# A hybrid decoder layer on one Trainium2 core: adaLN row sums on VectorE, a load order turned over five pairs, and a reordered ending

## The chip, the core and the metric

The kernel runs on one core of a Trainium2 chip. The core has five engines that run their own instruction streams and meet at semaphores: TensorE (PE, matrix products, with PEld for its weight loads), VectorE (DVE), ScalarE (ACT), GpSimd (POOL) and SyncE (SP, which here only issues DMAs). Sixteen DMA engines move data between HBM and the on-chip memory SBUF; products land in PSUM, which has eight banks of 512 float32 per partition. The metric is the device time of one execution in microseconds (us). Lower is better.

## What is computed

One decoder layer on 256 tokens of width 1024, float32 throughout. All weights are read once from HBM. Cut to what matters:

```
mod = c @ w_ada + b_ada                       # six rows of 1024: sh1, sc1, gt1, sh2, sc2, gt2
h = rms_norm(x, g1) * (1 + sc1) + sh1
proj = h @ w_in                               # DeltaNet q/k/v, z, FoX q/k/v, two gates
y_a = gated_deltanet(proj) @ w_o_delta        # chunked recurrence, 4 heads, 4 chunks of 64
y_b = forgetting_attention(proj) @ w_o_fox    # 4 heads
x = x + gt1 * ((sig(gate_a) * y_a + sig(gate_b) * y_b) @ w_out)
h2 = rms_norm(x, g2) * (1 + sc2) + sh2
x = x + gt2 * experts(h2)                     # router, top 4 of 32, clamped SwiGLU
out = rms_norm(x, g_final)
```

The conditioning `mod` has three parts of 2048 columns each, called ada0, ada1 and ada2 in the kernel: ada0 is sh1 and sc1, ada1 is gt1 and sh2, ada2 is sc2 and gt2. Each expert has 8 MB of gate and up weights and 4 MB of down weights, so the 32 experts are 403 MB of the 463 MB that are read.

## The kernel before

The order of all work is written by hand, one block of code for each engine. There is a first phase (to about 320 us), in which the layer up to the router is computed, and an expert phase.

**First phase.** The weights come through a ring of eight slots of 1 MB (`NSTREAM`), in the order of the list `UNITS`. `stream(n)` on SP issues the load of unit n once the unit that was in its slot has been used (`unit_used`, counted by PE). The list before: ada0 (8 units), dn (6), fqk (4), fv (2), z (2), ada1 (8), gates (8), ada2 (8), wo_fox (2), wo_delta (2), w_out (4). PE computes a conditioning part with `ada(part, b, ks)`: four products of 512 columns for each unit, with c copied into 32 columns as the weights, into four quarters of bank b. DVE then copies the bank (`take_mod_rows`), PE transposes the copy (`mod_transposes`), and DVE adds the bias (`take_mod`).

Projections (`project`) take a unit as two halves. For most units ACT rounds the weights (`w_hi`, line 1097), POOL computes the remainder (`w_lo`, line 1787, one operation of 128x1024 for each half, both inputs in SBUF), and PE makes three passes. DVE meanwhile does the convolution of the dn units, the decay and softmax biases, the scaling of q and k (lines 1448 and 1450) and the decay masks (lines 1457 and 1458, then `dec_ready`). PE waits for `dec_ready` before it transposes v (line 683), and after that projects z. Then come `chunk_pairs`, the triangular inverse by five levels with half a gates projection in each gap, and the recurrence over four chunks. The recurrence has more PE work in its gaps: `between_state` and `between_vnew`, the last three of which are ada2. After it, four calls of `out_branch` for wo_fox, four for wo_delta, and the product with w_out.

**Expert phase.** Experts go in pairs; pair I has experts 2I (par 0) and 2I+1 (par 1). PE, for each expert: gate and up products (`gate_up`, 8 units of 1 MB, lines 944 and after), transposes of the activation, then `down` in two halves of 2 MB. The gate and up weights have 16 slots (8 for each par), the first down half one place for each par, and the second half ("high", slots 18 and 19) one place that every expert uses in turn. SP's order of loads follows `by_place` up to pair 9: four gate-up loads of 2 MB, the first down half, and after them the high half of the expert before, since its place comes free last. From pair `TURN + 1 = 11` it follows `by_need`, where the high half of an expert comes directly behind its first half. Pair 10 is written out as the turn. Each load waits for its place to be free (`gu_used`, `dn_used`), and SP issues strictly in order.

**The ending.** `last_pair` multiplies the last expert's down weights into PSUM bank 6 after DVE has taken the expert before out of that bank (`y_moved`). `last_scatter` adds the last pair to the tokens. Then the final norm: ACT squares and roots, DVE one reciprocal and two products of 128x512 for each half of the tokens (line 1775), and ACT issues the four stores (line 1328).

## Time and profile before

| | us |
|---|---|
| median of three runs | 1239.37 |
| lowest, highest | 1239.18, 1241.2 |
| the profiled execution, its own time | 1238.21 |
| span of the profiled execution | 1236.4 |
| PE busy | 1138.6 (92%) |
| DVE busy | 316.1 (26%) |
| ACT busy | 184.7 (15%) |
| POOL busy | 106.0 (9%) |
| DMA | 464.7 MB, mean 376 GB/s |
| chain that ended last | PE 64%, DMA 29%, issue 3%, ACT 2%, DVE 2% |

The span is what lies between the first and the last instruction of the profiled execution, 1.8 us less than that execution's own time and 3.0 us less than the median. Times in rows are counted from the start of the span. "Idle before" is what an engine stood still for before a row's first instruction, with the name of what ended it. PE's clock as granted was 0.984 of full speed on average.

### The profile page before, as it was taken

The page shows a single profiled execution, that of the slowest core. Times are in us where ns is not written, and L with a number is a line of the kernel's source. Part 1 is how long each engine was busy: PE and PEld are TensorE (multiplying, and loading weights), DVE is VectorE, ACT ScalarE, POOL GpSimd, SP SyncE. Part 2 cuts the span into 40 slices and gives each one's busy share as a digit, 9 for nine tenths or more (in the row PEclk, how much of TensorE's full clock was granted, in tenths as well). Part 3 has the DMA queues.
Part 4 walks back from the last instruction along what each step waited for, and adds up shares of the span by engine and source line. Part 5 has one row for each costly group of instructions (what it writes and reads, how often), then busy time and mean ns, then how long its engine had stood idle before and what let it go on. Part 6 is the DMA issues. An engine that isn't in the chain of part 4 may idle for free.

```text
span 1236.4 us, 15283 instructions
## 1 busy us (share of the span) xinstructions
PE 1138.6 (92%) x6307; PEld 585.6 (47%) x6307; DVE 316.1 (26%) x674; ACT 184.7 (15%) x316; POOL 106.0 (9%) x50
## 2 busy tenths in 40 slices
PE   5999999999999999998989889898999999999896
PEld 2999799688543334333333323333434333333322
DVE  1633562131421221221212212121221222122102
ACT  2476344101310000010100000000000000000001
POOL 0764443110000000000000000000000000000000
PEclk9999999999999999999989999999999999999999
DMA  9963763597999999999999999999989999999995
GB/s 352 335 222 107 249 219 103 170 422 310 376 420 426 429 428 429 428 429 428 429 429 428 428 428 428 429 428 429 429 368 430 428 429 428 429 428 428 429 426 245
DMA packets 62558, 464.70 MB, mean 376 GB/s; under 512 B 8469, under 2 KB 31130, under 8 KB 34618
## 3 DMA queue, kind: packets, MB, share of 16 engines
q1 hardware_dynamic: 61256, 462.13, 90.9%
q10 hardware_dynamic: 1218, 1.93, 0.5%
q8 instruction: 26, 0.43, 0.1%
q0 software_dynamic: 48, 0.13, 0.0%
q14 instruction: 10, 0.08, 0.0%
HBM read 463.13 MB, written 1.05 MB: 375 GB/s over the span
## 4 chain that ended last, share of the span: by engine, by line
PE 64%; DMA 29%; issue 3%; ACT 2%; DVE 2%; SPq 0%; ACTq 0%; DVEq 0%
PE ps L488 61%; DMA ring<-in_w_down_dram 22%; DMA ring<-in_w_gate_up_dram 6%; PE ps L940 1%; ACT kept L1291 1%; DMA ring<-in_w_in_dram 1%; DMA ring<-in_g_onorm_dram 1%; PE ps L972 0%; PE ps L496 0%; ACT w_hi L1097 0%; DVE ring L1491 0%; SPq L358 0%; DVE ring L1485 0%; DVE ring L1775 0%; DVE kept L1717 0%
## 5 line engine op out<-in xcount | busy, mean ns | idle before, releaser
L488 PE MATMUL ps<-ring,kept 128*64 128x512 f32 (+1 forms) x3040 | 657.8, 600 | 36.1 <-DMA ring<-in_w_down_dram 22.5
L488 PEld LDWEIGHTS ps<-ring,kept 128*64 128x64 f32 (+1 forms) x3040 | 212.2, 138 | 454.3 <-issue 400.8
L488 PE MATMUL ps<-kept 128*128 128x128 f32 (+4 forms) x984 | 193.9, 413 | 8.5 <-ACT kept L1291 3.3
L488 PEld LDWEIGHTS ps<-kept 128*128 128x128 f32 (+2 forms) x984 | 108.5, 177 | 96.1 <-issue 81.0
L1287 ACT ACTIVATE kept<-kept 128x512 f32<-128x512 f32 x32 | 20.1, 629 | 731.4 <-DVE kept L1694 731.4
L1717 DVE TENSOR_TENSOR kept<-ps,kept 64x512 f32<-64x512 f32 x64 | 44.0, 688 | 298.4 <-PE ps L488 297.4
L1694 DVE TENSOR_SCALAR kept<-ps 128x512 f32<-128x512 f32 x32 | 22.1, 691 | 382.4 <-PE ps L488 382.4
L1787 POOL TENSOR_TENSOR w_lo<-ring,w_hi 128x1024 fp32r<-128x1024 f32 x38 | 91.8, 2434 | 108.2 <-ACT w_hi L1097 108.2
L488 PE MATMUL ps<-hT_hi,w_hi 128*128 128x256 f32 x272 | 78.7, 289 | 0.0
L488 PE MATMUL ps<-ring 64*64 64x64 f32 (+6 forms) x784 | 74.8, 270 | 3.0 <-issue 3.0
L488 PE MATMUL ps<-hT_lo,w_hi 128*128 128x256 f32 x272 | 77.0, 283 | 0.0
L488 PE MATMUL ps<-hT_hi,w_lo 128*128 128x256 f32 x272 | 76.9, 283 | 0.0
L488 PEld LDWEIGHTS ps<-ring 64*64 64x64 f32 (+3 forms) x784 | 65.4, 159 | 12.8 <-issue 6.9
L488 PE MATMUL ps<-kept,ring 128*128 128x256 f32 (+1 forms) x252 | 56.2, 381 | 4.7 <-DMA ring<-in_w_in_dram 2.6
L488 PEld LDWEIGHTS ps<-kept,ring 128*128 128x128 f32 x252 | 47.1, 195 | 12.3 <-issue 3.3
L488 PEld LDWEIGHTS ps<-hT_hi,w_hi 128*128 128x128 f32 x272 | 52.1, 192 | 0.5
L488 PEld LDWEIGHTS ps<-hT_lo,w_hi 128*128 128x128 f32 x272 | 52.1, 192 | 0.1
L488 PEld LDWEIGHTS ps<-hT_hi,w_lo 128*128 128x128 f32 x272 | 52.1, 192 | 0.0
L1097 ACT ACTIVATE w_hi<-ring 128x1024 fp32r<-128x1024 f32 x38 | 39.2, 1053 | 49.2 <-PE ps L488 37.1
L940 PE MATMUL ps<-kept 128*128 128x128 f32 x128 | 21.7, 292 | 22.6 <-issue 22.6
L940 PEld LDWEIGHTS ps<-kept 128*128 128x128 f32 x128 | 19.1, 206 | 33.4 <-issue 29.3
L1291 ACT ACTIVATE kept<-ps 128x512 f32<-128x512 f32 x32 | 19.1, 597 | 85.7 <-PE ps L940 85.7
(227 smaller groups left out, 513.8 us busy)
## 6 DMA issues: line engine op xcount, KB each, us to landing
ring<-in_w_gate_up_dram SPq DMA_DIRECT2D x127, 2048.0 KB, 26.4
ring<-in_w_down_dram SPq DMA_DIRECT2D x47, 2048.0 KB, 23.8
kept<-in_w_down_dram SPq DMA_DIRECT2D x16, 2048.0 KB, 24.0
ring<-in_w_ada_dram SPq DMA_DIRECT2D x24, 1024.0 KB, 5.0
ring<-in_w_in_dram SPq DMA_DIRECT2D x22, 1024.0 KB, 11.5
ring<-in_w_out_dram SPq DMA_DIRECT2D x4, 1024.0 KB, 16.3
ring<-in_w_o_fox_dram SPq DMA_DIRECT2D x2, 1024.0 KB, 9.8
ring<-in_w_o_delta_dram SPq DMA_DIRECT2D x2, 1024.0 KB, 12.8
```

The source lines that it names most:

```text
L488: return pe.matmul(dst, lhsT, rhs, start=start, stop=stop, skip_group_check=True)
L940: last = pe.transpose(bank(7, kk * P, P), fours[:, kk, :], ident)
L1097: A(hi_buf_r(n)[:, :, cols], w[:, :, cols], ACT.Copy).then_inc(S("split_hi"), 1)
L1287: A(sig_a, gate_a, ACT.Sigmoid, scale=ALPHA).then_inc(S("sig_ready"), 1)
L1291: A(act_t_last if par == 0 and not more else act_t, bank(7), ACT.Copy).then_inc(S("act_t_ready"), 1)
L1694: TS(gate_a, bank(4), LIMIT, None, ALU.min).then_inc(S("gate_ready"), 1)
L1717: TTn(ypair[par * 64:par * 64 + 64, d * 512:(d + 1) * 512], ps[64 * d:64 * d + 64, 6, :], gt2_row[64 * d:64 * d + 64, d * 512:(d + 1) * 51 ...
L1787: pool.tensor_tensor(lo_r[:, :, cols], lo[:, :, cols], hi_buf_r(n)[:, :, cols].bitcast(F32), ALU.subtract).then_inc(S("split_lo"), 1)
```

## The change

Conditioning. The eight units of ada1 and of ada2 are no longer multiplied by PE. DVE builds a sum over them (`add_rows`): a unit of 128x2048 times c as a scalar for each partition, added to `ada_sums[part]`, sixteen operations in all, of which the first of each part is a product alone. Each counts `ada_used`. PE then adds the 128 rows with four products against a matrix of ones (`ada_over_rows`, counts `ada_summed`), one for each quarter of the bank. The units of ada1 and ada2 are spread over the list `UNITS` from the third dn unit to the z units, and a slot that held one is released by `ada_used`. `mod_transposes(1)` moves ahead of the chunk pairs, and the one of ada2 from behind the recurrence to ahead of the levels, which now wait for `mod_cols_taken` 3. The gaps of the recurrence that held ada2 hold the first two `fox_branch` calls.

Load order. `next_expert(I, i, par, late)` replaces `by_place` and `by_need`: `late` says behind how many loads of this expert the high half of the expert before is placed. It is 5 up to pair 8 and then 4, 3, 2, 1, 0, 0 for pairs 9 to 14.

Ending. The last expert's down goes to bank 4, with a wait for `gate_up_taken` in place of `y_moved`. In the final norm one of the four quarters is multiplied by g_final before its root is there and scaled by ACT; three stores go out from SP and one from ACT. Some semaphores are merged, without an effect on the order.

The diff, cut to its core:

```diff
-        UNITS += [("dn", u, win_unit(256 * u)) for u in range(6)]
...
-        UNITS += [("ada1", k, ada_unit(1, k)) for k in range(KD)]
...
+        UNITS += [dn(0), dn(1), dn(2), ada(1, 0), dn(3), dn(4), ada(1, 1), dn(5), fox(0), ada(1, 2), ada(1, 3)]
+        UNITS += [fox(1), fox(2), ada(1, 4), ada(1, 5), ada(1, 6), fox(3), ada(1, 7), ada(2, 0), fox(4), ada(2, 1)]
+        UNITS += [ada(2, 2), fox(5), ada(2, 3), ada(2, 4), zz(0), ada(2, 5), zz(1), ada(2, 6), ada(2, 7)]
...
-                    sp.wait_ge(S("unit_used"), n - NSTREAM + 1)
+                    sp.wait_ge(S("ada_used" if SUMMED[n - NSTREAM] else "unit_used"),
+                               USED_AT[UNITS[n - NSTREAM][0:2]])
...
+            def next_expert(I, i, par, late, first_unit_whole=True):
...
+                for u in range(4):
+                    if u == late:
+                        high_of_last()
...
+                next_dn(I, i, par, 0)
+                if late == 5:
+                    high_of_last()
...
+                for i, late in zip(range(TURN, PAIRS - 1), (4, 3, 2, 1, 0, 0)):
...
+            def ada_over_rows(part, b):
+
+                pe.wait_ge(S("ada_used"), KD * part)
+                for q in range(4):
+                    last = mm(ps[32 * q:32 * q + 32, b, :], km("ones")[:, 0:32],
+                              ada_sums[part][:, 512 * q:512 * q + 512], True, True)
+                last.then_inc(S("ada_summed"), 1)
...
+            def add_rows(part, k):
...
+                if k == 0:
+                    last = TS(ada_sums[part], unit_sb(n), vec("c", k), None, ALU.mult)
+                else:
+                    dve.wait_ge(S("ada_used"), KD * (part - 1) + k)
+                    last = STT(ada_sums[part], unit_sb(n), vec("c", k), ada_sums[part], ALU.mult, ALU.add)
...
-                pe.wait_ge(S("y_moved"), i * 4 + 2)
-                down(i, 1, high, last_of=q)
+                pe.wait_ge(S("gate_up_taken"), i * 4 + 4)
+                down(i, 1, high, last_of=q, to=4)
...
+            act.wait_ge(S("norm_steps"), 4)
+            link(A(x2[:, 1, 0:512], x2[:, 1, 0:512], ACT.Copy, scale=oss[:, 1, 1:2]))
+            act.dma_start(out[0, P:2 * P, 0:512], x2[:, 1, 0:512]).then_inc(S("out_done"), 16)
```

**On DVE, before the decay masks.** The rows stand between the copy of the cumulated decays (128x48) and the first decay mask. `ring<-ring,kept 128x2048` is `add_rows`; a semaphore in brackets is what the instruction waits for, `slot_in` for a load. Before:

```order
L1429 COPY kept<-ps 128x48 [waits cums_ps]
L1436 SCALAR_TENSOR_TENSOR kept<-ps,kept,ring 128x128 [waits cums_ps,cums_taken]
L1438 SCALAR_TENSOR_TENSOR kept<-ps,kept,ring 128x256
...
L1448 SCALAR_TENSOR_TENSOR ring<-ring 128x1024 [waits qk_rstd,rowF_taken]
L1450 TENSOR_TENSOR ring<-ring 128x1024 [waits qk_rstd]
L1457 SCALAR_TENSOR_TENSOR ring<-ps,kept,ring 128x128 [waits cums_ps,unit_qk]
```

Now:

```order
L1474 COPY kept<-ps 128x48 [waits cums_ps]
L1427 SCALAR_TENSOR_TENSOR ring<-ring,kept 128x2048 [waits ada_used,slot_in5]
L1427 SCALAR_TENSOR_TENSOR ring<-ring,kept 128x2048 [waits ada_used,slot_in6]
...
L1427 SCALAR_TENSOR_TENSOR ring<-ring,kept 128x2048 [waits ada_used,slot_in1]
L1424 TENSOR_SCALAR ring<-ring,kept 128x2048 [waits slot_in2]
L1427 SCALAR_TENSOR_TENSOR ring<-ring,kept 128x2048 [waits ada_used,slot_in4]
...
L1427 SCALAR_TENSOR_TENSOR ring<-ring,kept 128x2048 [waits ada_used,slot_in0]
L1498 SCALAR_TENSOR_TENSOR ring<-ring 128x1024 [waits qk_rstd,rowF_taken]
L1500 TENSOR_TENSOR ring<-ring 128x1024 [waits qk_rstd]
```

Three operations of 128x2048 now stand ahead of the softmax biases (128x128 and 128x256), and six between them and the scaling of q and k.

**On PE, from the end of the z projections to the inverse's levels.** `128x12`, `128x64` and the `128x128` beside them are `mod_transposes`, `64x64` the chunk pairs, `32x512` a product with a conditioning unit or sum. Before:

```order
L488 MATMUL ps<-ring 64x64 [waits tok_taken]
...
L488 MATMUL ps<-ring,kept 32x512 [waits slot_in6,rowF_taken]
L488 MATMUL ps<-ring,kept 32x512 x3
L488 MATMUL ps<-ring,kept 32x512 [waits slot_in7]
...
L513 MATMUL ps<-kept 128x12 [waits run_in,mod_rows_sb]
...
L700 MATMUL ps<-kept,ring 128x128 [waits X1_ready]
```

Now:

```order
L536 MATMUL ps<-kept 128x12 [waits run_in,mod_rows_sb]
...
L503 MATMUL ps<-ring 64x64 [waits tok_taken]
...
L503 MATMUL ps<-ring,kept 32x512 [waits ada_used,mod_cols_taken]
L503 MATMUL ps<-ring,kept 32x512 x3
...
L725 MATMUL ps<-kept,ring 128x128 [waits X1_ready]
...
L538 MATMUL ps<-kept 128x128 [waits mod_rows_sb]
...
L503 MATMUL ps<-ring 128x128 [waits U_ready,M_ready,attn_ready,mod_cols_taken]
```

The 32 products of ada1 are gone from between the pairs and the transposes of X, the first half gates projection stands there in their place, and the first level waits for the conditioning's last part.

**On PE, at the end of the recurrence.** `128x256` from `ring` alone is an `out_branch`. Before:

```order
L488 MATMUL ps<-ring,kept 32x512 [waits slot_in6,obT_ready]
...
L488 MATMUL ps<-ring 64x128 [waits state_ready]
...
L488 MATMUL ps<-ring,kept 32x512 [waits slot_in1]
...
L488 MATMUL ps<-ring 128x256 [waits proj_taken,slot_in7,slot_in6]
L488 MATMUL ps<-ring 128x256 x7
L515 MATMUL ps<-kept 128x128 [waits mod_rows_sb]
```

Now:

```order
L503 MATMUL ps<-ring 128x256 [waits slot_in7,proj_taken,slot_in6,obT_ready]
L503 MATMUL ps<-ring 128x256 x7
L503 MATMUL ps<-ring 64x128 [waits state_ready]
...
L503 MATMUL ps<-ring 128x256 [waits proj_taken,slot_in7,slot_in6]
L503 MATMUL ps<-ring 128x256 x7
L503 MATMUL ps<-ring 128x128 [waits vnew_ready]
L503 MATMUL ps<-ring 128x128 x3
L503 MATMUL ps<-ring 128x256 [waits slot_in7,slot_in6,yb_taken]
```

Two of the four branches with wo_fox have moved into the gaps of the recurrence, where ada2 stood.

## Rows read from the trace of the kernel before

**Rows 1.** Windows: length; PE, PEld, DVE, ACT, POOL busy; PEclk, DMA share, GB/s

```profile
241.00:301.50 60.50, 57.51 (x286) 48.39 (x279) 16.11 (x31) 2.82 (x11) 7.79 (x5) 0.97 1.01 411
301.50:311.00 9.50, 9.50 (x58) 8.15 (x57) 1.77 (x5) 3.12 (x6) 0.00 (x0) 1.00 0.02 7
311.00:485.00 174.00, 165.24 (x822) 69.86 (x822) 45.87 (x123) 21.22 (x43) 1.60 (x2) 1.00 1.00 422
485.00:886.00 401.00, 365.84 (x1690) 142.33 (x1686) 84.19 (x189) 27.69 (x56) 0.00 (x0) 0.97 1.01 429
...
914.00:922.00 8.00, 8.00 (x40) 2.67 (x38) 2.78 (x7) 0.00 (x0) 0.00 (x0) 1.00 0.54 188
```

**Rows 2.** Timeline of SP's issues (start, us, count)

```profile
266.05 45.02 SPq L358 DMA_DIRECT2D ring<-in_w_gate_up_dram  x8
...
918.85 0.33 SPq L373 DMA_DIRECT2D ring<-in_w_down_dram  x1
```

**Rows 3.** Timeline of DVE, 24 to 124 us

```profile
24.65 2.29 DVE L1351 TENSOR_TENSOR kept<-kept 128x2048 f32<-128x2048 f32 x1 [9.57 <-ACT kept L1083]
...
94.51 0.21 DVE L1429 COPY kept<-ps 128x48 f32<-128x48 f32 x1 [0.62 <-PE ps L488]
100.74 0.35 DVE L1436 SCALAR_TENSOR_TENSOR kept<-ps,kept,ring 128x128 f32<-128x128 f32 x1 [6.02 <-PE ps L488]
...
116.90 1.23 DVE L1448 SCALAR_TENSOR_TENSOR ring<-ring 128x1024 f32<-128x1024 f32 x1 [13.46 <-ACT ring L1174]
...
123.18 0.34 DVE L1458 SCALAR_TENSOR_TENSOR ring<-ps,kept,ring 128x128 f32<-128x128 f32 x1
```

**Rows 4.** Timeline of POOL

```profile
93.38 5.03 POOL L1787 TENSOR_TENSOR w_lo<-ring,w_hi 128x1024 fp32r<-128x1024 f32 x2 [1.07 <-ACT w_hi L1097]
109.32 4.77 POOL L1787 TENSOR_TENSOR w_lo<-ring,w_hi 128x1024 fp32r<-128x1024 f32 x2 [10.92 <-ACT w_hi L1097]
118.76 9.82 POOL L1787 TENSOR_TENSOR w_lo<-ring,w_hi 128x1024 fp32r<-128x1024 f32 x4 [4.67 <-ACT w_hi L1097]
145.80 9.41 POOL L1787 TENSOR_TENSOR w_lo<-ring,w_hi 128x1024 fp32r<-128x1024 f32 x4 [17.23 <-ACT w_hi L1097]
...
178.92 5.22 POOL L1787 TENSOR_TENSOR w_lo<-ring,w_hi 128x1024 fp32r<-128x1024 f32 x2 [4.02 <-ACT w_hi L1097]
```

**Rows 5.** Timeline of DVE, products with both inputs in SBUF

```profile
124.35 1.89 DVE L1465 TENSOR_TENSOR kept<-kept 128x8 f32<-128x8 f32 x1 [0.83 <-issue]
...
178.38 3.51 DVE L1491 TENSOR_TENSOR ring<-ring 128x512 f32<-128x512 f32 x2 [0.84 <-PE ps L488]
```

**Rows 6.** Timelines of PE and ACT, 123 to 155 us

```profile
123.58 1.09 PE L683 MATMUL ps<-kept,ring 128*128 128x128 f32 x8 [1.37 <-DVE ring L1458]
...
136.11 2.08 PE L488 MATMUL ps<-ring 128*64 128x64 f32 x64
138.12 7.08 PE L488 MATMUL ps<-ring,kept 128*32 128x512 f32 x64
...
154.86 0.60 ACT L1131 ACTIVATE ring<-ps 128x512 f32<-128x512 f32 x1 [2.72 <-PE ps L488]
```

**Rows 7.** Timeline of PE, 234 to 259 us

```profile
234.84 2.78 PE L488 MATMUL ps<-ring,kept 128*32 128x512 f32 x24
237.55 1.96 PE L488 MATMUL ps<-ring 128*64 128x128 f32 x16
...
248.15 5.38 PE L488 MATMUL ps<-ring 128*128 128x256 f32 x16 [2.99 <-issue]
...
254.52 3.72 PE L488 MATMUL ps<-ring 128*128 128x256 f32 x16
```

**Rows 8.** Timeline of all engines, 1216 to 1233 us

```profile
1216.92 3.65 PE L488 MATMUL ps<-kept 128*64 128x512 f32 x16 [1.51 <-DVE kept L1717]
...
1221.69 0.14 PEld L488 LDWEIGHTS ps<-ring,kept 128*64 128x64 f32 x2 [0.29 <-DMA ring<-in_w_down_dram]
...
1230.79 1.41 DVE L1775 SCALAR_TENSOR_TENSOR ring<-ps,kept,ring 128x512 f32<-128x512 f32 x2
```

More of the change, by code:

```diff
@@ L281, in layer_kernel @@
         UNIT_AT = {(name, i): n for n, (name, i, _) in enumerate(UNITS)}
+        SUMMED = [name in ("ada1", "ada2") for name, _, _ in UNITS]
+        USED_AT = {(name, i): SUMMED[:n + 1].count(SUMMED[n]) for n, (name, i, _) in enumerate(UNITS)}
         WHOLE = 1
@@ L481, in _ @@
             sp.wait_ge(S("gu_used"), n * (16 * PAIRS) + (16 * PAIRS - 8))
[L482 removed]
+            sp.dma_start(flat[:, 0:1024], g_final.partition_broadcast(P)).then_inc(S("narrow_in"), 16)
+            for t, d, step in ((0, 0, 3), (0, 1, 5), (1, 1, 6)):
+                cols = slice(512 * d, 512 * d + 512)
+                sp.wait_ge(S("norm_steps"), step)
+                sp.dma_start(out[0, t * P:(t + 1) * P, cols], x2[:, t, cols]).then_inc(S("out_done"), 16)
         @block.tensor
@@ L497, in _, with ada @@
                 last.then_inc(S("x_t"), 1)
-            def ada(part, b, ks=range(KD)):
+            def ada(b, ks=range(KD)):
                 for k in ks:
-                    w = unit_arrived(pe, f"ada{part}", k)
+                    w = unit_arrived(pe, "ada0", k)
                     for q in range(4):
@@ L523, in _ @@
             pe.wait_ge(S("cb_ready"), 1)
-            ada(0, 4, range(2))
+            ada(4, range(2))
             pe.wait_ge(S("xsq_ready"), 1)
@@ L529, in _ @@
             last.then_inc(S("xss_ps"), 1)
-            ada(0, 4, range(2, KD))
+            ada(4, range(2, KD))
             mod_transposes(0, 6)
@@ L941, in act_transposes, with down @@
                 last.then_inc(S("act_t_ps"), 1)
-            def down(i, par, high, js=range(2), acts=None, last_of=None):
+            def down(i, par, high, js=range(2), acts=None, last_of=None, to=6):
                 e = i * 2 + par
@@ L1430, in _ @@
             ins.then_inc(S("cums_taken"), 1)
+            for k in range(4, 7):
+                add_rows(1, k)
             dve.wait_ge(S("cums_taken"), 1)
@@ L1440, in _ @@
             last.then_inc(S("rowF_taken"), 1)
+            add_rows(1, 7)
+            for k in range(5):
+                add_rows(2, k)
             dve.wait_ge(S("rowF_taken"), 1)
@@ L1480, in _ @@
             last.then_inc(S("tok_taken"), 1)
+            for k in range(5, KD):
+                add_rows(2, k)
+            take_mod_rows(1, 5)
+            take_mod(1, 6)
             dve.wait_ge(S("pairs_ps"), 1)
```

211 lines of the change are left out of this document (108 added, 103 removed).

## The prediction

> **What bounds the kernel now.** Read first where the DMA engines stand still. From 311 to 485 us they move 422 GB/s, from 485 to 886 us 429 GB/s at a share of 1.01 [rows 1], while PE has gaps: it is busy 365.84 of 401 us. The expert phase is therefore bound by the stream of weights, and PE's own work there costs nothing. The stream has two holes. One is before it: from 301.5 to 311 us the DMA share is 0.02 [rows 1]. SP has a batch of eight gate-up loads under way, from 266.05 to 311.07 us [rows 2]; the last two wait for PE to finish the product with w_out, as PE is busy all through the hole. All that comes later is a fixed number of bytes, so each us by which PE's first phase ends earlier or later moves the end by a us. The second hole is at 914 to 922 us, share 0.54 [rows 1]: (1.01 - 0.54) x 8 = 3.8 us, at the turn of the load order, and it ends when SP issues a high half at 918.85 us [rows 2]. Behind the last byte there is a tail that PE, DVE and ACT make. So three things count: the length of PE's first phase, the hole at the turn, the tail.
>
> **The first phase: DVE's new work.** The price of one addition of 128x2048 with two inputs in SBUF is 2.29 us, from a product of that size [rows 3]; a three-operand operation of 128x1024 takes 1.23 us [rows 3], which fits. The two operations of part start (one input) are not in the trace: 2.3 us if they run at the same pace, about 1.3 if at the double; I take 1.3. Sixteen operations are some 35 us, most of it where DVE is idle. Four of them lie between convolutions, one more or less fills a gap each, and nobody waits for DVE there. Three follow the copy at 94.51 us, which has 6.02 us of idle time behind it, and six follow the softmax biases, with 13.46 us of idle time [rows 3]. By their own length: from 94.7 us three additions (6.9), the biases (2.7), 2.3 + 1.3 + 4 x 2.3 = 12.8, scaling of q and k (2.4), masks (4.2) end at 123.7 us. Before, the masks end at 123.52 us [rows 3]. So if these operations ran alone, this would cost 0.2 us.
>
> They don't run alone. POOL has eight of its remainders just here: two from 93.38, two from 109.32, four from 118.76 us, 2.4 us each [rows 4]. DVE's products with both inputs in SBUF take turns with such a POOL operation. A product of 128x8 takes 1.89 us, from 124.35 to 126.24, in the middle of POOL's run of four [rows 5]; two of 128x512 take 3.51 us, where 2048 elements alone take 2.29, and POOL's pair beside them takes 5.22 us against 4.77 [rows 4, 5]. One waits for the whole of the other's operation, and neither gets two in a row while the other waits. No row shows the three-operand form with two SBUF inputs beside a working POOL; the two that bound it are that product (full turn-taking) and the same form at 116.90 us with POOL idle (none) [rows 3]. I take the turn-taking, since the inputs are the same two. The Trainium skill states this as a rule (SBUF — State Buffer, "Who interferes with whom"): a DVE instruction with two SBUF inputs and a GpSimd instruction that reads SBUF exclude each other for a whole instruction. By that rule the cost is the one taken here; the trace agrees for the two-operand form.
>
> The sum: DVE reaches its first addition at 94.7, when POOL's first operation has some 1.3 us left; the other seven come in between one by one, 7 x 2.37 = 16.6 us. Masks then end at 123.7 + 17.9 = 141.6 us instead of 123.52. PE waits for them (1.37 us already now [rows 6]), so its z projections start **18.1 us later**. Its clock falls after such a stop: behind a wait of 2.99 us a branch of 16 records takes 5.38 us and the same one later 3.72 [rows 7], so 1.7 us more. The four products for ada1 between the z units cost 7.08 / 8 = 0.9 us [rows 6]. Sum at the end of z: **+20.7 us**.
>
> **From z to the levels.** Now it takes from 136.1 us (the start of the pairs) to 154.8 us (ACT takes gates 0, the last PE work before the levels) [rows 6], 18.7 us, of which ada1 is 7.08. That goes, 0.9 for ada2's sum comes. But two waits come with it. The gates 0 and 1 units arrive earlier than now, so ACT and POOL split them directly behind z, not from 145.80 us [rows 4]: POOL's four operations then stand across DVE's four products of level 0 and X, which take turns with them. Each waits up to 2.4 us; X is ready some 3.3 us after PE's gates 0. And DVE copies ada2's sum only after level 1, the attention product and q's decay (about 4.3 us from X on), PE transposes it (1.2) and DVE takes it (0.4) before the first level may start, where PE has only 1 us of other work. My sum from z's end: transposes 1.6, pairs 2.1, sum 0.9, gates 0 5.9, wait 3.3, then 5.9, together 19.7 us. **+1.0 us.**
>
> **The recurrence and the branches.** From 234.84 us, the first piece of ada2, to the fourth branch, at which SP issues again (266.05), it is 31.2 us now [rows 2, 7]. In it: ada2 (7.1), the wait of 2.99 for wo_fox, the slow branch, the transposes. What is left is 4 branches x 3.72, 1.96 and 1.16 of recurrence, 1.04 of transposes: 19.0 us. The wait for wo_fox goes, as its slots are now freed by gates units. What is late next is the root of the recurrence's norm, some 4.3 us after the recurrence, and 5.6 us of branches cover it. **-12.2 us.**
>
> First phase in all: 20.7 + 1.0 - 12.2 = **+9.5 us**.
>
> **The turn.** Between two high halves there are six loads (29.3 us at 4.9 us each); a step of `late` makes it five, once for each pair. A pair is then 11 loads, 53.8 us, and PE's own pair of experts is about as long, so neither waits. The high place is free about 6 us after its last load landed, with four or five loads (20 to 25 us) still under way. So the hole goes: **-3.8 us**, bounded by 0.
>
> **The ending.** The last down no longer waits 1.51 us for DVE [rows 8]. Its last load still lands shortly before 1221.7 us [rows 8], which may take back a part: -1.2, between -0.3 and -1.5. In the norm, one of the four products of 0.7 us [rows 8] leaves the path, and the four stores are no longer issued one behind the other: -1.2, between -0.5 and -1.8.
>
> **Sum, the likeliest case.** +9.5 - 3.8 - 2.4 = +3.3 us, rounded up to +3.6 for waits too small to list. The profiled execution's span is 1236.4 us, its own time 1238.21, the median 1239.37. Against the median: **1243 us**. Its own range: the turn-taking may cost 13 to 20 us instead of 18, the rest 3 us either way: 1238 to 1248.
>
> **Rivals.**
> *Three-operand additions don't take turns with POOL.* Then z starts 0.2 to 1.5 us later; DVE still has three additions ahead of ada1's transposes, which makes PE wait some 1.5 us; X is still late against POOL. The levels start about 2 us later than now, and the sum is +2 - 12.2 - 3.8 - 2.4 = -16.4: **1223 us** (1219 to 1230). For it: no row shows the form beside POOL. Against it: the two-operand rows. It decides at the first addition behind 94.7 us: 2.3 us or about 3.6.
> *The turn has a hole of its own*, or leaves the old one. For it: SP issues strictly in order, and every step puts a wait for `dn_used` earlier. Against it: the loads under way. Then 1243 + 3.8 = **1247 us**.
> *The first phase doesn't count.* If the hole of 9.5 us before the stream could take up a later end of w_out, the change would give only turn and ending: 1239.4 - 6.2 = 1233 us. Against it: the last two loads of the batch wait for that very product, and the hole grows with it.
>
> **How the numbers follow.** Measurement of this kernel can tell about 0.2%, 2.5 us. Likeliest case 0.63 (of it slower 0.39, same 0.19, faster 0.05); additions without turns 0.23, faster; a hole at the turn 0.08, slower; first phase without effect 0.02, faster; 0.04 for what I don't see, half same, half slower. Faster 0.30, same 0.21, slower 0.49. The range of 8 in 10 takes in the middle of the second case: 1221 to 1248.
>
> **What would show it.** Right: additions of 2.3 us that measure 3.5 to 4.7 where POOL works; a PE wait of some 15 to 19 us before line 683's transposes; masks done near 141.6 us; levels near 176 us; gate-up batch done near 320 us; no window under a share of 0.95 between 330 us and the end of the stream. Wrong: additions that stay at 2.3 us at 95 to 130 us, a z start before 130 us, or a new wait of PE for down weights in pairs 9 to 14.

## The result, and the profile after

The changed kernel takes 1245.2 us in the median of 20 executions (1240.13 to 1248.22), the kernel before 1238.99 us (20 executions, 1237.37 to 1242.17). The ratio is 1.0046, with a 95% interval of 1.0036 to 1.0055: slower by 5.7 us by the ratio (the two medians lie 6.2 us apart), where the forecast was +3.6 us and 1243 us. The profiled execution took 1242.11 us with a span of 1240.1 us, 3.7 us more than the span of before (1236.4). It lies 3.1 us under its own median; why is one of the questions below.

The page's line of the chain that ended last says where the new time is. DVE's share was 2%, now it is 5%, and PE's is the same:

```profile
PE 64%; DMA 25%; DVE 5%; issue 3%; ACT 2%; ACTq 0%; SPq 0%; DVEq 0%
```

Windows of the changed kernel (length; PE, PEld, DVE, ACT, POOL busy; PEclk, DMA share, GB/s), against [rows 1]:

```profile
301.00:311.00 10.00, 10.00 (x61) 8.56 (x59) 1.75 (x4) 0.40 (x1) 0.00 (x0) 1.00 1.01 429
311.00:321.00 10.00, 9.52 (x60) 8.09 (x56) 1.45 (x4) 3.73 (x9) 0.38 (x1) 1.00 0.41 143
485.00:886.00 401.00, 371.56 (x1717) 144.03 (x1715) 82.93 (x185) 27.49 (x56) 0.00 (x0) 0.97 1.01 428
914.00:922.00 8.00, 7.70 (x37) 2.64 (x36) 0.05 (x1) 0.60 (x1) 0.00 (x0) 1.00 1.00 426
```

SP's batch of eight gate-up loads in the changed kernel (start, us):

```profile
273.88 45.12 SPq L373 DMA_DIRECT2D ring<-in_w_gate_up_dram  x8
```

The batch is done at 319.00 us against 311.07 in [rows 2], so the hole ahead of the stream of weights, in which the DMA engines stand nearly still, has moved from between 301.5 and 311 us to between some 313 and 319 us, and is shorter. Between 485 and 886 us the stream is what it was, and the hole at 914 to 922 us (share 0.54 in [rows 1]) is gone (1.00). The last load lands shortly before 1225.48 us, 3.8 us later than in [rows 8]: 7.9 us lost ahead of the stream, 4.1 won at the turn. The tail behind it is as long as before.

Where the 7.9 us come from. DVE in the changed kernel, 96 to 138 us, to be laid beside [rows 3]:

```profile
96.02 9.50 DVE L1427 SCALAR_TENSOR_TENSOR ring<-ring,kept 128x2048 f32<-128x2048 f32 x3
...
108.05 2.35 DVE L1427 SCALAR_TENSOR_TENSOR ring<-ring,kept 128x2048 f32<-128x2048 f32 x1
110.31 1.28 DVE L1424 TENSOR_SCALAR ring<-ring,kept 128x2048 f32<-128x2048 f32 x1
111.69 15.53 DVE L1427 SCALAR_TENSOR_TENSOR ring<-ring,kept 128x2048 f32<-128x2048 f32 x4
127.15 3.36 DVE L1498 SCALAR_TENSOR_TENSOR ring<-ring 128x1024 f32<-128x1024 f32 x1
130.43 3.36 DVE L1500 TENSOR_TENSOR ring<-ring 128x1024 f32<-128x1024 f32 x1
...
137.70 0.34 DVE L1508 SCALAR_TENSOR_TENSOR ring<-ps,kept,ring 128x128 f32<-128x128 f32 x1
```

POOL in the same stretch, against [rows 4]:

```profile
94.21 6.72 POOL L1845 TENSOR_TENSOR w_lo<-ring,w_hi 128x1024 fp32r<-128x1024 f32 x2 [1.57 <-ACT w_hi L1127]
111.29 6.95 POOL L1845 TENSOR_TENSOR w_lo<-ring,w_hi 128x1024 fp32r<-128x1024 f32 x2 [10.37 <-ACT w_hi L1127]
120.72 15.28 POOL L1845 TENSOR_TENSOR w_lo<-ring,w_hi 128x1024 fp32r<-128x1024 f32 x4 [2.49 <-ACT w_hi L1127]
```

An addition alone takes 2.35 us (108.05). Four of them from 111.69 us take 15.53, 3.88 each, and the scaling of k, 1.22 us alone, takes 3.36. POOL's operations stretch as well: four take 15.28 us where they took 9.82. The masks end at 138.04 us instead of 123.52, and PE has to wait for them and for what stands ahead of them:

```profile
133.84 0.47 PE L700 MATMUL ps<-kept,ring 128*128 128x128 f32 x1 [9.47 <-DVE ring L1500]
...
138.10 1.97 PE L706 MATMUL ps<-kept,ring 128*128 128x128 f32 x8 [2.29 <-DVE ring L1508]
...
166.53 1.09 PE L725 MATMUL ps<-kept,ring 128*128 128x128 f32 x8 [2.67 <-DVE ring L1551]
170.79 1.11 PE L538 MATMUL ps<-kept 128*128 128x128 f32 x4 [3.17 <-DVE kept L1403]
...
172.91 3.78 PE L503 MATMUL ps<-ring 128*128 128x128 f32 x16 [0.34 <-DVE kept L1394]
```

The last row is the first level of the inverse: 3.78 us for 16 products of 128x128, half as fast as before, when the same row was

```profile
154.66 1.95 PE L488 MATMUL ps<-ring 128*128 128x128 f32 x16
```

PE's clock is at its lower level there. The windows of the changed kernel over PE's waits show that:

```profile
124.00:134.00 10.00, 0.53 (x5) 0.33 (x4) 9.96 (x4) 2.79 (x5) 10.00 (x4) 0.68 1.05 372
134.00:139.00 5.00, 2.71 (x12) 2.31 (x13) 4.96 (x19) 0.92 (x1) 2.01 (x1) 0.50 0.60 190
139.00:146.50 7.50, 7.50 (x58) 7.37 (x60) 7.40 (x7) 2.42 (x4) 0.00 (x0) 0.85 0.00 0
146.50:153.40 6.90, 6.90 (x57) 5.93 (x51) 3.00 (x3) 0.56 (x2) 0.00 (x0) 1.00 0.88 268
153.40:163.90 10.50, 10.46 (x130) 9.09 (x130) 8.18 (x14) 5.66 (x7) 8.89 (x4) 1.00 1.02 320
163.90:173.00 9.10, 2.96 (x17) 2.21 (x17) 8.24 (x12) 0.59 (x1) 1.42 (x1) 0.76 0.34 122
173.00:186.00 13.00, 13.00 (x103) 12.61 (x104) 4.16 (x5) 2.14 (x3) 2.37 (x1) 0.78 0.00 1
```

A PEclk of 0.50 is 1.2 GHz, 1.00 is 2.4 GHz; values between are mixtures. There are two dips, one in and behind the waits for k and the masks (9.47 and 2.29 us) and one in and behind the two waits ahead of the levels (2.67 and 3.17 us). The second one was not in the forecast.

### The profile page after: what moved, and what is told of

It reads as the page before. It is cut to its first block, busy times and chain, and to the rows that moved or that the text cites. A ratio compares the mean times of both kernels' runs of the same rounds, so it can differ in the third digit from the quotient of the medians.

```text
span 1240.1 us, 14937 instructions
## 1 busy us (share of the span) xinstructions
PE 1134.3 (91%) x6195; PEld 588.6 (47%) x6195; DVE 377.3 (30%) x690; ACT 185.4 (15%) x317; POOL 122.0 (10%) x50
## 3 DMA queue, kind: packets, MB, share of 16 engines
HBM read 463.13 MB, written 1.05 MB: 374 GB/s over the span
## 4 chain that ended last, share of the span: by engine, by line
PE 64%; DMA 25%; DVE 5%; issue 3%; ACT 2%; ACTq 0%; SPq 0%; DVEq 0%
PE ps L503 61%; DMA ring<-in_w_down_dram 14%; DMA ring<-in_w_gate_up_dram 6%; DMA kept<-in_w_down_dram 4%; DVE ring L1427 2%; PE ps L970 1%; ACT kept L1321 1%; DMA ring<-in_w_in_dram 1%; DMA ring<-in_g_onorm_dram 1%; DVE ring L1545 0%; PE ps L1002 0%; PE ps L511 0%; DVE ring L1498 0%; DVE ring L1551 0%; DVE ring L1500 0%
## 5 line engine op out<-in xcount | busy, mean ns | idle before, releaser
L503 PE MATMUL ps<-ring,kept 128*64 128x512 f32 (+2 forms) x2928 | 643.1, 598 | 32.1 <-DMA ring<-in_w_down_dram 18.2
L503 PEld LDWEIGHTS ps<-ring,kept 128*64 128x64 f32 (+2 forms) x2928 | 208.5, 138 | 440.9 <-issue 393.9
L503 PE MATMUL ps<-kept 128*128 128x128 f32 (+4 forms) x984 | 197.5, 420 | 8.3 <-ACT kept L1321 3.3
L1845 POOL TENSOR_TENSOR w_lo<-ring,w_hi 128x1024 fp32r<-128x1024 f32 x38 | 107.8, 2860 | 113.4 <-ACT w_hi L1127 113.4
L1427 DVE SCALAR_TENSOR_TENSOR ring<-ring,kept 128x2048 f32<-128x2048 f32 x14 | 46.4, 3316 | 0.9
```

The lines of the kernel that those rows point to most:

```text
L503: return pe.matmul(dst, lhsT, rhs, start=start, stop=stop, skip_group_check=True)
L1427: last = STT(ada_sums[part], unit_sb(n), vec("c", k), ada_sums[part], ALU.mult, ALU.add)
L1845: pool.tensor_tensor(lo_r[:, :, cols], lo[:, :, cols], hi_buf_r(n)[:, :, cols].bitcast(F32), ALU.subtract).then_inc(S("split_lo"), 1)
```

## The experiments

### The three parts, each alone

```diff
 turn_only: the kernel before, with
-    TURN = 10
+    TURN = 9
+                for i, late in zip(range(TURN, PAIRS - 1), (4, 3, 2, 1, 0, 0)):
 ending_only: the kernel before, with
+                pe.wait_ge(S("gate_up_taken"), i * 4 + 4)
+                down(i, 1, high, last_of=q, to=4)
+            TTn(x2[:, 1, 0:512], bank(2), flat[:, 0:512], ALU.mult).then_inc(S("norm_steps"), 1)
+            for t, d, step in ((0, 0, 3), (0, 1, 5), (1, 1, 6)):
 cond_only: the changed kernel without these two
```

> The kernel before with the new load order alone. Theory (the hole at 914 to 922 us of the kernel before goes, and everything behind it moves up by its length): 3.8 us faster, ratio 0.9969, no window under a DMA share of 0.95 between 330 us and the end of the stream, batch of eight gate-up loads done at 311 us as before. Rival (the new order gains nothing by itself: the hole goes elsewhere, and the profiled execution of the changed kernel was short for another reason): 0 to 1 us, ratio 0.999 to 1.000.

> The kernel before with the new ending alone: last down in bank 4, one quarter of the norm shared with ACT, three stores from SP. Theory (as the two traces stand): the last down's wait for DVE is replaced by one for its own weights, and the norm's shorter DVE work is given back where SP issues three stores one behind the other: 0 us, between -0.5 and +0.5, ratio 0.9996 to 1.0004; the time from the last down product's end to the end of the span stays at 12.3 us. Rival (the forecast's terms hold, and other things hid them in the changed kernel): 1.2 to 2.4 us faster, ratio 0.998 to 0.999.

> The changed kernel with the old load order and the old ending, so the conditioning alone. Theory (the end follows the first phase one to one): the batch of eight gate-up loads is done near 319 us against 311.07, and the median is 8 to 10 us above that of the kernel before, ratio 1.0065 to 1.008; the single executions differ by some 8 us from each other and the longer ones have the lower mean clock. Rival (the conditioning costs less than 6 us, and turn and ending gave nothing or took something in the changed kernel): ratio under 1.005.

| | median, us | ratio to before, interval |
|---|---|---|
| before, beside these | 1238.58 | |
| turn_only | 1234.47 | 0.9966 (0.9953 to 0.9979) |
| ending_only | 1238.97 | 1.0004 (0.9995 to 1.0012) |
| cond_only | 1249.14 | 1.0087 (1.0069 to 1.0105) |

The turn gives 4.1 us, the ending nothing (its median is 0.4 us higher, within the interval), the conditioning costs 10.6. The three differences of medians add up to 6.8 us, against 6.2 for the whole change. The window of the turn, in turn_only:

```profile
914.00:922.00 8.00, 8.00 (x40) 2.66 (x38) 1.84 (x6) 0.00 (x0) 0.00 (x0) 1.00 1.01 430
```

So for turn and ending the theory held each time. For the conditioning 8 to 10 us and a batch near 319 us were expected; it cost more, though the lower end of the interval lies in that range. In cond_only the profiled execution shows a pattern that the changed kernel's did not. Its DVE, same stretch:

```profile
95.55 11.03 DVE L1429 SCALAR_TENSOR_TENSOR ring<-ring,kept 128x2048 f32<-128x2048 f32 x3
109.10 2.34 DVE L1429 SCALAR_TENSOR_TENSOR ring<-ring,kept 128x2048 f32<-128x2048 f32 x1
111.36 3.42 DVE L1426 TENSOR_SCALAR ring<-ring,kept 128x2048 f32<-128x2048 f32 x1
114.89 15.50 DVE L1429 SCALAR_TENSOR_TENSOR ring<-ring,kept 128x2048 f32<-128x2048 f32 x4
```

The first three take 11.03 us instead of 9.50, and the product at 111 us, which has one input only, 3.42 instead of 1.28. Masks end at 141.21 us, the batch is done at 321.90. The order in which DVE and POOL arrive decides how often one waits for the other. Here the product starts 1.05 us later and POOL's operation 0.73 us earlier (110.56 instead of 111.29) than in the changed kernel, so POOL's is ahead of it. And the first addition, which in the changed kernel meets only the last 0.5 us of an operation of POOL and takes 2.69 us, starts almost together with that operation and waits for the whole of it.

### Is it the turn-taking, or the additions' own length?

```diff
 small_lo: the changed kernel, with
+                    if 9 <= n < BEFORE_GATES:
+                        cols = slice(m * P, m * P + 1)
                     pool.tensor_tensor(lo_r[:, :, cols], lo[:, :, cols], hi_buf_r(n)[:, :, cols].bitcast(F32),
...
+                if 9 <= ns < BEFORE_GATES:
+                    lo = hi
 small_adds: the changed kernel, with
-                    last = STT(ada_sums[part], unit_sb(n), vec("c", k), ada_sums[part], ALU.mult, ALU.add)
+                    last = STT(ada_sums[part][:, 0:64], unit_sb(n)[:, 0:64], vec("c", k), ada_sums[part][:, 0:64],
+                               ALU.mult, ALU.add)
```

> The changed kernel with POOL's remainders of the four units fv and z (eight operations between 94 and 136 us) cut to one column of each 128, and PE taking the rounded weights twice instead of the remainder, so these projections are not computed exactly. Everything else, DVE's sixteen operations included, stays. Theory (DVE's additions take turns with POOL): the additions from 96 us on measure 2.3 us each instead of 3.2 to 3.9, masks end near 125 us instead of 138.0, PE starts z near 126 us instead of 139.7, batch done near 305 us instead of 319.0, time 12 to 14 us shorter than the changed kernel's: about 1232 us. Rival (the additions' own length or the arrival of their units sets the masks): masks end at 132 us or later, time 1239 us or more.

> The changed kernel with the fourteen accumulating additions cut to 64 of 2048 columns (the conditioning sums are not computed), the two products of 2048 columns kept. It shows what the changed order of loads, PE's and POOL's work costs or gains without DVE's new work. Theory: masks end near 123 us, z starts near 125 us, the batch is done near 304 us, 14 to 15 us before the changed kernel's, time about 1231 us, the same within 2 us as with POOL's remainders cut, as the additions fit into DVE's idle time. Rival (own length counts beside the turns): this one is 5 us or more shorter than the one with POOL's remainders cut.

With POOL's eight operations out of the way the additions run at their own length. DVE in small_lo:

```profile
95.06 7.26 DVE L1429 SCALAR_TENSOR_TENSOR ring<-ring,kept 128x2048 f32<-128x2048 f32 x3
...
108.48 9.72 DVE L1429 SCALAR_TENSOR_TENSOR ring<-ring,kept 128x2048 f32<-128x2048 f32 x4
118.12 1.22 DVE L1500 SCALAR_TENSOR_TENSOR ring<-ring 128x1024 f32<-128x1024 f32 x1
```

All fourteen additions, with the shortest, the middle and the longest duration in ns, in the changed kernel and, in the second fence, in small_lo:

```profile
L1427 DVE SCALAR_TENSOR_TENSOR ring<-ring,kept x14: 2342/3399/4299, 61.9 to 146.7; 128x2048 f32<-128x2048 f32 x14
```

```profile
L1429 DVE SCALAR_TENSOR_TENSOR ring<-ring,kept x14: 2339/2351/3344, 62.7 to 135.0; 128x2048 f32<-128x2048 f32 x14
```

Masks end at 124.75 us, the batch is done at 304.68 us, the time is 1229.4 us (ratio 0.9928, 0.9913 to 0.9943): 14.3 us earlier at the batch than the changed kernel, and 14.6 us less by the two ratios, where 12 to 14 were expected. In small_adds masks end at 124.02 us and the batch is done at 303.42 us. Its whole time (2171.65 us) can't be compared, since without the sums the router sends more tokens to one expert than a round holds, and the expert phase runs twice. The two batches are 1.3 us apart, so the additions' own length costs about that, and the turn-taking, with the lower clock behind the longer waits, some 14 us. Without it the changed conditioning gains 6.4 us in the first phase (304.68 against 311.07), although this kernel also spares POOL the work itself.

### PE's clock, and why executions differ

```diff
 kept_busy and kept_busy2: the changed kernel, with
+            def keep_busy(b, n):
+                for _ in range(n):
+                    mm(bank(b), hT_hi_r[:, 0, 0:P], hT_hi_r[:, 0:2, :], True, True)
+
+            pe.wait_ge(S("qk_ss_taken"), 1)
+            keep_busy(6, 38)
             pe.wait_ge(S("unit_qk"), 2)
-            pe.wait_ge(S("qk_ss_taken"), 1)
...
+            keep_busy(6, 8)
             pe.wait_ge(S("dec_ready"), 1)
...
+            keep_busy(5, 10)
             pe.wait_ge(S("X1_ready"), 1)
...
+            keep_busy(5, 11)
             mod_transposes(2, 6)
```

> The changed kernel with products into an unused bank in four of PE's waits between 124 and 171 us (38, 8, 10 and 11 products of 128x512), so that PE is not idle there; they end before the waits do. Theory (behind each stop PE runs at the lower granted clock, and how long differs from execution to execution): PEclk 1.00 instead of 0.82 from 136 to 180 us, the first z unit in 6.0 us instead of 6.7, levels begin 2 to 4 us earlier, batch done near 315 us, median 3 to 6 us below the changed kernel's: 1240 us, and the executions within 3 us of each other instead of 8. Rival (the spread has another source): batch at 316 to 319 us, a spread of 8 us again, median 1243 to 1245 us.

> The changed kernel itself, unedited, for another profiled execution beside the next run. Theory (how many of POOL's operations come in between DVE's differs from execution to execution): this execution either repeats the first profile (three additions from 96 us in 9.5 us, the product at 110 us in 1.28 us, masks done at 138.0 us, batch of eight gate-up loads done at 319 us) or the pattern of the run with the conditioning alone (11.0 us, 3.42 us, 141.2 us, 322 us), and nothing between; its own time stands 3 to 4 us above the first one's in the second case. Median about 1245 us. Rival (the executions differ through PE's clock alone): masks done within 0.5 us of 138.0 us again, whatever the time.

> The same kernel as the run with PE kept busy in four waits, now timed beside the changed kernel on the same chip. Theory: 4 to 5 us less from the end of the masks to the end of the batch of gate-up loads (176.3 us in the first such run against 181.0 in the changed kernel), and so a median 3 to 5 us below that of the changed kernel timed beside it. Rival (the stream gives it back, or the gain in one profile was chance): within 1.5 us of the changed kernel.

PE's clock stays at 1.00 in kept_busy2, in the windows that stood at 0.76 and 0.78 in the changed kernel, and it is 1.00 in all windows from 120 to 163.9 us as well, where the first dip was:

```profile
163.90:173.00 9.10, 7.66 (x44) 5.93 (x43) 7.81 (x12) 0.08 (x1) 0.98 (x1) 1.00 0.33 118
173.00:186.00 13.00, 13.00 (x149) 12.40 (x148) 5.26 (x7) 3.56 (x5) 2.37 (x1) 1.00 0.06 6
```

| profiled execution | masks end, us | batch done, us | between |
|---|---|---|---|
| changed kernel | 138.04 | 319.00 | 180.96 |
| changed_again | 138.03 | 319.08 | 181.05 |
| cond_only | 141.21 | 321.90 | 180.69 |
| kept_busy | 140.66 | 316.99 | 176.33 |
| kept_busy2 | 139.01 | 315.34 | 176.33 |

The last column is steady within 0.4 us with the dips and to the hundredth without them: they cost 4.5 us. The first column is not steady: four values over 3.2 us. The changed kernel itself repeated its 138.0 us, so the second pattern was seen only in kernels edited elsewhere (cond_only has the same code up to there, and kept_busy and kept_busy2 differ from it ahead of the masks only in PE's added products). With kept_busy2 in between, the expectation of two patterns and nothing between doesn't hold for them, and neither does the rival that puts all the difference on the clock. The rows show two parts: where DVE's first addition starts (94.17 to 96.09 us), and what the turns add to its own length (12.3 us in the two of the changed kernel, 15.2 in kept_busy2, 15.9 and 16.1 in cond_only and kept_busy). The medians follow only in part: kept_busy 1243.62 us (ratio 1.0040, 1.0026 to 1.0054), kept_busy2 1242.5 (1.0029, 1.0015 to 1.0042), changed_again beside it 1244.5 (1.0050, 1.0034 to 1.0065). That is 2 us where 3 to 5 were expected, with intervals that overlap; for the first of the two kernels 1240 us had been expected. The spread of single executions was 3.8 and 4.6 us, and 6.3 us for changed_again.

A part of the other 2 to 3 us can be seen in the profiles. From the batch's end to the end of the span it is 923.7 us in kept_busy and 922.9 in kept_busy2, but 921.1 and 919.9 in the two executions of the changed kernel. Between 5 and 15 us behind the batch PE's clock is 0.66 and 0.83 in the first two and 1.00 in the others, with the same three waits of PE behind the batch (0.5, 1.3 and 1.0 us) in all four. The other kernels divide in the same way (small_adds aside, which runs the expert phase twice). With the new turn the remainder is 922.7 to 923.7 us in the five profiled executions with that dip and 919.9 to 921.1 in the four without; with the old turn it is 927.8 in ending_only, with the dip, and 924.5 to 925.3 in the three without. The clearest pair is late_sum2 (922.8) and late_sum3 (920.7), two kernels of a later section that differ only in their stores and whose batches end at 304.85 and 304.83 us. Windows: length; PE busy; PEclk, DMA share, GB/s

```profile
309.85:319.85 10.00, 8.21 (x48) 0.83 1.01 403
```

```profile
309.83:319.83 10.00, 8.20 (x56) 1.00 1.00 413
```

Why the clock falls there in one execution and not in another, and whether it is the cause of the 2 to 3 us, no run shows. The two profiles of kept_busy also have later masks than the two of the changed kernel, and a few of each don't settle whether that is their rule.

### The ending once more

```diff
 ending_two_two: ending_only, with
-            for t, d, step in ((0, 0, 3), (0, 1, 5), (1, 1, 6)):
+            for t, d, step in ((0, 0, 3), (1, 1, 6)):
...
+            act.wait_ge(S("norm_steps"), 5)
+            act.dma_start(out[0, 0:P, 512:1024], x2[:, 0, 512:1024]).then_inc(S("out_done"), 16)
```

> The kernel before with the new ending, but two stores from SP and two from ACT instead of three and one; SP issues the first and the last quarter, ACT the two between. Theory (the third store in a row on one queue takes 1.46 us to issue instead of 0.34, and the last quarter waits for just that): SP's last issue is over 0.35 to 0.45 us after DVE's last product instead of 1.5 us, the time from the end of PE's last down product to the end is 11.3 us instead of 12.4, and the median is 1 us below that of the run with the new ending alone: ratio 0.999 to 1.000. Rival (the third issue was slow because the transfers before it filled the engines, and the landing follows that): no change, ratio 1.0004.

In the changed kernel DVE needs 3.33 us from the mean squares (1231.98 us) to the end of its last product (1235.31), where it needed 3.95 before (1228.25 to 1232.20); then comes SP's last store. SP's three stores and PE's last down in the changed kernel, from its timeline:

```profile
1220.65 3.65 PE L503 MATMUL ps<-kept 128*64 128x512 f32 x16 [1.36 <-DMA kept<-in_w_down_dram]
...
1233.78 0.34 SPq L497 DMA_DIRECT2D out_dram<-ring  x1
1234.68 0.34 SPq L497 DMA_DIRECT2D out_dram<-ring  x1
1235.34 1.46 SPq L497 DMA_DIRECT2D out_dram<-ring  x1
```

The wait for DVE of 1.51 us in [rows 8] has become one of 1.36 us for the down weights: bank 4 is free in time, the data are not there. And the third store from SP takes 1.46 us to issue. I took that for the cost of a third issue in a row on one queue. In ending_two_two no queue has three, and the SP and ACT rows are:

```profile
1230.61 0.35 SPq L486 DMA_DIRECT2D out_dram<-ring  x1
...
1231.91 1.32 ACTq L1331 DMA_DIRECT2D out_dram<-ring  x1
1232.17 1.06 SPq L486 DMA_DIRECT2D out_dram<-ring  x1
```

Both second stores end their issue at 1233.23 us, to within 0.01 us, on two queues. The median is 1238.43 us, the ratio 1.0003 (0.9993 to 1.0014), as for ending_only. My theory is wrong, and the rival fits better: something that the two queues share holds the later issues back. It has no fixed time. Counted from the start of the first store's issue, the held one ends after 2.62 us here, 3.02 in the changed kernel and 2.94 before (ACT's third issue began at 1231.58 and took 1.42 us), but after 1.89 us in late_sum3 and 1.81 in kept_busy; and in cond_only, with the old ending, none of the four takes more than 0.52 us. What it is, no run shows. DVE's part of the norm became 0.62 us shorter, and in the medians nothing of it arrives.

### A version that keeps the good part

The gain behind the recurrence doesn't need DVE's work where POOL's is. In these three kernels PE multiplies ada1 as in the kernel before, and only ada2 is summed on DVE, one or two units at a time in its gaps in the levels and the recurrence, into two tiles of 128x1024 that are free there; the turn and the ending stay.

```diff
+        UNITS += [ada(1, k) for k in range(KD)]
+        UNITS += [("gates", u, win_unit(COL_GATES + 256 * u)) for u in range(6)]
+        UNITS += [ada(2, k) for k in range(KD)]
+        UNITS += [("gates", u, win_unit(COL_GATES + 256 * u)) for u in range(6, 8)]
...
-                            2: lambda: fox_branch(0), 3: lambda: None}
+                            2: lambda: fox_branch(0), 3: lambda: ada_over_rows(6)}
...
 late_sum2, DVE in the levels (late_sum: add_rows(0) ahead of them, {1: (1,), 5: (2, 3)})
+                for k in {4: (0,), 5: (1, 2)}.get(s, ()):
+                    add_rows(k)
                 dve.wait_ge(S("XR_ps"), s)
 late_sum3: late_sum2 with the stores of ending_two_two
```

> The changed kernel, but ada1 is multiplied by PE again at its old place, and only ada2 is summed on DVE, one unit each in gaps of DVE in the levels and the recurrence in which POOL is mostly idle; no addition stands before the decay masks. Two branches with wo_fox stay in the gaps of the recurrence. The sum is held in two halves, so an addition is two operations of 128x1024. Theory (the loss is DVE's additions taking turns with POOL ahead of the masks, and the gain of 12 to 13 us behind the recurrence does not depend on them): masks end near 123.5 us, recurrence starts near 205 us as in the kernel before, batch done near 299 us, stream and end 12 us earlier and 3.8 for the turn: about 1223 us, ratio 0.987. Rival 1 (the transfers from 240 us on become the bound, as the DMA share there is 1.01 in the kernel before, so only the hole of 9.5 us can be gained): about 1226 us, ratio 0.989. Rival 2 (additions in the levels delay the levels as much as they gain): 1233 us or more.

> The kernel of the run before with the sum of ada2 late in the recurrence, but the first addition no longer stands where its load has not landed: it moves from ahead of level 2 (where DVE stood still 12.87 us for that load and PE 4.94 us for DVE) to the fourth level, and the others follow one gap later each. Theory: PE's levels run as in the kernel before, recurrence starts near 205 us against 213.2, batch of eight gate-up loads done near 302 us against 310.4, median 8 us below that run: 1227 us, ratio 0.991. Rival (transfers from 240 us on are the bound): no better than 1230 us.

> The kernel with ada2's sum late in the recurrence (second form) and the stores two by two. Theory: 1 us below that run's ratio of 0.9932, so 0.9924, about 1229 us. Rival (the stores gain nothing): 0.9932.

late_sum took 1235.38 us (ratio 0.9971, 0.9960 to 0.9982), no more than the turn alone gives. Its DVE and PE rows show why:

```profile
164.34 0.75 DVE L1428 TENSOR_SCALAR ring<-ring,kept 128x1024 f32<-128x1024 f32 x1 [12.87 <-DMA ring<-in_w_ada_dram]
```

```profile
173.08 1.98 PE L504 MATMUL ps<-ring 64*64 64x64 f32 x32 [4.94 <-DVE ring L1575]
```

The first addition stood where its load had not landed, so DVE did nothing for 12.87 us, and the levels had to wait. I had looked at when the slot comes free, not at when the load lands, some 11 us after its issue at 152.92 us. With the additions moved on by some gaps, late_sum2 takes 1230.03 us (0.9932, 0.9918 to 0.9945). Its batch:

```profile
259.64 45.21 SPq L374 DMA_DIRECT2D ring<-in_w_gate_up_dram  x8
```

It is done at 304.85 us, 5.8 us before turn_only's (310.63); 302 was expected. Part of the rest is PE's new wait of 1.53 us for the branches of wo_fox at 250.30 us. And DVE still meets POOL: the two products that start the sum take 2.89 and 2.92 us beside its remainders, where late_sum's take 0.75, one addition takes 3.43 and another, beside POOL's sum of the rounded parts, 5.32 instead of 1.28. The median lies 3 us above the 1227 us of the theory, and just where the rival had its bound (no better than 1230 us). But the rival's reason, transfers that are the limit, has little for it in the trace: the DMA share is 0.31 between 296 and 305 us. late_sum3 takes 1228.46 us (0.9922, 0.9906 to 0.9938), which can't be told from late_sum2. Both beat the kernel before, by 8 to 10 us, and the changed one, by 14 to 17.

## Why the prediction was right, and where it was not

| step of the forecast | forecast | profiled execution | rests on |
|---|---|---|---|
| masks end | 141.6 us (+18.1) | 138.04 (+14.5); 138.0 to 141.2 in five | DVE rows |
| clock behind that wait | +1.7 | +1.6 (from v's transposes to the end of the first z unit 6.7 before, 8.3 now) | PE rows |
| ada1's sum between the z units | +0.9 | +1.06 | PE rows |
| end of z to the first level | +1.0 | +1.1 (18.48, now 19.55) | PE rows |
| first level | 0 | +2.8 (9.26, now 12.09) | second dip of the clock |
| from there to the batch's end | -12.2 | -13.2 (147.15, now 134.00) | PE and SP rows |
| **first phase** | **+9.5** | **+7.9; +10.6 as cond_only's median** | |
| turn | -3.8 | -4.1 | turn_only |
| ending | -2.4 | 0 | ending_only |
| **sum** | **+3.3** | **+3.7 in the span, +5.7 by the ratio** | |

**What held.** The expert phase is bound by its stream, and the first phase moves the end one to one, to within some 2 us either way: from the batch's end to the end of the span it is 919.9 to 923.7 us in the profiled executions with the new turn, and 924.5 to 927.8 in those with the old one. So the rival by which the first phase doesn't count is out. One reason that I gave against it was wrong, though: the hole does not grow with a later w_out, it shrank from 9.5 us to some 6, as the loads ahead of it were later too; what moved is the end of the batch. The additions do take turns with POOL. That was argued from the two-operand rows in [rows 4, 5] and is now shown for the three-operand form (3.88 us against 2.35) and by small_lo, where the cost goes away with POOL's work. The rule that was cited from the Trainium skill (SBUF — State Buffer, "Who interferes with whom") agrees here too. The rival without turns (1223 us, 1219 to 1230) is near what small_lo shows, where the turns are gone, 1229.4 us; the changed kernel is far from it. The turn has no hole of its own: in turn_only and in the changed kernel no stretch of 8 us from 330 us to 1210 us is under a DMA share of 0.95.

**The masks, too late by 3.6 us in the profile.** I let the rest of POOL's first operation and all seven others come in between, 2.37 us each. In the changed kernel DVE's first addition starts 1.3 us later than I had it (96.02 us), so only 0.35 us of POOL's first operation, over at 96.56 us, is left to wait for. Six operations come in between, of about 2 us each for DVE (an addition takes 4.3 us instead of 2.35). The eighth runs from 132.67 to 136.01 us, mostly beside the masks, whose inputs come in part from PSUM and which are not slowed (0.34 and 0.35 us). In all the turns add 12.3 us, where I had 17.9; that is just under the 13 to 20 us of my range. In cond_only they add 15.9 us, eight turns, and the masks end at 141.21 us, my figure within 0.4 us, with one turn on an operation that I had taken to be free of them: the product with one input. One sign that I had named was missed for this reason: PE's waits ahead of the transposes of v are 9.47 and 2.29 us, together 11.8, not 15 to 19. Besides the earlier masks, PE itself came to the wait 3 us later than before (its last product with an fv unit ends at 124.37 instead of 121.3 us). In cond_only the two waits are 16.1 us.

**The second dip of the clock, not foreseen.** I priced one stop, the long one, from a row behind the recurrence [rows 7]. I listed the waits for X and for ada2's columns ahead of the levels, but did not ask what PE's clock does behind them. It cost 2.8 us in the first level, a term that my sum had at nothing. The two kernels with PE kept busy show both dips together at 4.5 us.

**The ending, the step that failed.** The forecast of -2.4 us had two terms, and in ending_only nothing came of either (ratio 1.0004, 0.9995 to 1.0012). For the last down I had the right warning in hand (its last load still lands shortly before 1221.7 us, [rows 8]) and took it for a part of the gain; it was all of it. For the norm I counted DVE's product as being on the path. DVE did become 0.62 us faster there, but the path goes on through the issue of the last store, which in the changed kernel and in ending_only was held (1.46 and 1.53 us) when DVE came earlier. [rows 8] ends at DVE's products; ACT's stores stood in the same timeline and I had not asked what ended their idle time.

**The numbers.** The two misses in the sum, +2.8 for the second dip and +2.4 for the ending, are together larger than the miss of 3.6 us on the masks on the other side, and the steps behind the levels took off another 1.0. That these misses nearly cancel, so that the span came out at +3.7 against +3.3, is luck. Against the median 2.2 us are left. Later masks than the profiled execution's, as in cond_only, would give them, but only a few executions were profiled, so that isn't shown. 1245.2 us lies inside 1221 to 1248, and inside the likeliest case's 1238 to 1248.

## What to carry to other kernels

Work that fits into an engine's idle time by its own length can still cost 14 us if another engine has to take turns with it at that time: lay the two timelines over each other before moving it, and choose a gap in which the other engine is idle and the operand has landed, not merely been asked for. When a change makes PE stop, price the stop twice, once for the wait and once for the products behind it at half the clock. And a gain at the very end counts only if the transfer behind it can start earlier. One profiled execution is not enough for steps of a few us: the same stretch behind the batch came out 2 to 3 us longer or shorter with PE's clock.

## What was not expected of the hardware

- A product of 128x2048 with one SBUF input and a scalar for each partition takes 1.28 us alone and took 3.42 us beside POOL: the form with one input takes turns as well. The Trainium skill says so (SBUF — State Buffer, "Who interferes with whom": a tensor_scalar can enter a mode that holds both ports); this case's row agrees, and my sum had left it out.
- An operation of POOL over 128x8 elements, 0.22 us alone, took 1.80 us beside an addition of DVE: the wait depends on what the other has under way, not on one's own size. From small_lo's timeline of POOL:

```profile
94.73 0.22 POOL L1849 TENSOR_TENSOR w_lo<-ring,w_hi 128x8 fp32r<-128x8 f32 x1 [2.00 <-ACT w_hi L1129]
95.67 1.80 POOL L1849 TENSOR_TENSOR w_lo<-ring,w_hi 128x8 fp32r<-128x8 f32 x1 [0.73 <-ACT w_hi L1129]
```

- The changed kernel's 20 executions span 8 us, and its longer ones have the lower mean clock (0.967 at 1248.22 us, 0.977 at 1240.13 us), where the 20 of the kernel before span 5 us. Four executions of small_lo, without the turns, span 1.3 us. So the turn-taking is the likely cause, with the different waits of PE and its clock behind them, but executions of different length were not profiled side by side to show it.
- Store issues on two queues, SP's and ACT's, were held up together and ended within 0.01 us of each other, 2.6 us after the first store in ending_two_two; the same pair in late_sum3 ended within 0.01 us too, but after 1.9 us.
- With the same three waits (0.5, 1.3 and 1.0 us), PE's clock behind the batch fell in some executions (0.66 in kept_busy, 0.83 in late_sum2) and not in others (1.00 in the changed kernel and in late_sum3).
